# An earlier first projection in the head, and routing that takes the sample tiles first and gathers from the residual stream

## The reference, cut to what matters

```python
mod = jax.nn.silu(cvec) @ p['w_ada'] + p['b_ada']
sh1, sc1, g1, sh2, sc2, g2 = [m[:, None, :] for m in jnp.split(mod, 6, axis=-1)]
h = _rms_norm(x, p['norm1_g']) * (1 + sc1) + sh1
mix, k, v = _mixing(h, p, kv_ctx)
x = x + g1 * mix
h2 = _rms_norm(x, p['norm2_g']) * (1 + sc2) + sh2
x = x + g2 * _expert_choice_ffn(h2, p)

...
logits = (h @ p['w_router']).astype(jnp.float32) + p['b_router'].astype(jnp.float32)
aff = jax.nn.softmax(logits, axis=-1)
gate, idx = lax.top_k(aff.transpose(0, 2, 1), cap)
xs = jax.vmap(lambda hb, ib: hb[ib])(h, idx)
gg = jnp.einsum('becd,edf->becf', xs, p['w_e_gate'])
uu = jnp.einsum('becd,edf->becf', xs, p['w_e_up'])
y = jnp.einsum('becf,efd->becd', jax.nn.silu(gg) * uu, p['w_e_down']) * gate[..., None].astype(h.dtype)
```

## Time and profile before

| | |
|---|---|
| median of three runs | 1210.63 us (1210.62 to 1211.57) |
| profiled execution | 1212.05 us |
| its span | 1209.6 us |
| mean granted TensorE clock | 0.995 |
| PE busy | 1179.1 us, 97% of the span |
| DVE, ACT, POOL busy | 898.7, 613.1, 283.5 us |
| moved by DMA | 303.25 MB, 251 GB/s on average |

### The profile page before, as it was taken

The page is one execution under the profiler, slowest core; times in us unless marked ns, Lnnn a source line. Parts: engine busy times, 40 slices in busy tenths (PEclk is TensorE's granted clock), DMA queues, the critical chain, the costliest instruction groups (busy, mean ns, idle before and its releaser), DMA issues.

```text
span 1209.6 us, 18766 instructions
## 1 busy us (share of the span) xinstructions
PE 1179.1 (97%) x7330; PEld 941.3 (78%) x7330; DVE 898.7 (74%) x1047; ACT 613.1 (51%) x710; POOL 283.5 (23%) x189
## 2 busy tenths in 40 slices
PE   5999999999999999999999999999999999999995
PEld 3788899988899999999995666666666666666663
DVE  2689674558877174237568999999999999999997
ACT  3421332245541351322124777777777777777774
POOL 1131030002201143333126212222222112222213
PEclk9999999999999999999999999999999999999998
DMA  9887726221213123444349999999999999999995
GB/s 339 295 240 234 248 64 157 85 99 35 73 36 105 36 71 100 161 158 153 111 174 369 388 379 378 378 380 381 381 386 389 381 377 378 380 381 380 381 387 202
DMA packets 154762, 303.25 MB, mean 251 GB/s; under 512 B 7363, under 2 KB 55527, under 8 KB 154706
## 3 DMA queue, kind: packets, MB, share of 16 engines
q1 hardware_dynamic: 141942, 271.76, 62.1%
q0 software_dynamic: 3968, 12.64, 4.7%
q10 hardware_dynamic: 8796, 18.05, 4.3%
HBM read 285.25 MB, written 17.18 MB: 250 GB/s over the span
## 4 chain that ended last, share of the span: by engine, by line
PE 90%; DVE 5%; issue 1%; DMA 1%; POOL 1%; ACT 0%; SPq 0%; POOLq 0%; ACTq 0%; DVEq 0%
PE bank L1812 17%; PE bank L1813 17%; PE bank L1814 17%; PE bank L1838 5%; PE bank L1841 5%; PE bank L1843 5%; PE bank L1840 5%; PE bank L1842 5%; PE bank L1839 5%; DVE fa L1236 3%; PE bank L2116 1%; DMA wring<-in_w_ada 1%; DVE fa L1328 1%; PE bank L2099 1%; PE bank L2329 1%
## 5 line engine op out<-in xcount | busy, mean ns | idle before, releaser
L1812 PE MATMUL bank<-h2r_a,xTh 128*80 128x512 f32 x368 | 145.4, 395 | 0.0
L1813 PE MATMUL bank<-l2r_b,xTh 128*80 128x512 f32 x368 | 144.7, 393 | 0.0
L1814 PE MATMUL bank<-h2r_a,xTl 128*80 128x512 f32 x368 | 143.4, 390 | 0.0
L693 POOL TENSOR_TENSOR half<-half 1x1 f32<-1x1 f32 x26 | 60.2, 2316 | 287.6 <-DVE ye L1772 286.6
L1236 DVE SCALAR_TENSOR_TENSOR fa<-fa,cwT 128x655 f32<-128x655 f32 x120 | 111.1, 967 | 0.9
L1058 ACT CAST h2r_a<-w_a 128x2048 fp32r<-128x2048 f32 x46 | 88.1, 1914 | 42.9 <-PE bank L1814 42.9
L589 POOL TENSOR_TENSOR lring<-wring,hring 128x2048 fp32r<-128x2048 f32 x15 | 70.2, 4681 | 162.5 <-ACT hring L752 162.5
L1623 DVE TENSOR_TENSOR l2r_b<-w_a,h2r_a 128x2048 fp32r<-128x2048 f32 x45 | 102.8, 2284 | 5.8 <-ACT h2r_a L1058 5.5
L1838 PE MATMUL bank<-hTh,hring 128*128 128x320 f32 x320 | 104.4, 326 | 1.7 <-DVE hTl L1296 0.8
L1843 PE MATMUL bank<-hTh,lring 128*128 128x320 f32 x320 | 98.8, 309 | 0.0
L1841 PE MATMUL bank<-hTl,hring 128*128 128x320 f32 x320 | 98.8, 309 | 0.0
(11 more groups left out here) (433 smaller groups left out, 3205.4 us busy)
## 6 DMA issues: line engine op xcount, KB each, us to landing
w_b<-in_w_e_down SPq DMA_DIRECT2D x48, 1024.0 KB, 14.8
w_e<-in_w_e_up SPq DMA_DIRECT2D x32, 1024.0 KB, 16.8
w_r<-in_w_e_gate SPq DMA_DIRECT2D x32, 1024.0 KB, 16.9
w_a<-in_w_e_gate SPq DMA_DIRECT2D x32, 1024.0 KB, 14.6
w_a<-in_w_e_up SPq DMA_DIRECT2D x32, 1024.0 KB, 14.3
wring<-in_w_in SPq DMA_DIRECT2D x20, 1024.0 KB, 5.1
w_a<-in_w_e_down SPq DMA_DIRECT2D x16, 1024.0 KB, 14.1
fa<-in_w_ada SPq DMA_DIRECT2D x14, 1024.0 KB, 9.0
```

Source lines behind the costliest of these rows:

```text
L1812: pe.matmul(out, lh, rh, start=start, stop=False)
L1813: pe.matmul(out, lh, rl, start=False, stop=False)
L1814: return pe.matmul(out, ll, rh, start=False, stop=stop)
```

## The change

It has two parts that do not touch each other.

**Head.** The order on PE is written anew: pair turns 0 and 1 come after turn 3, `turn_x(6)` before `ada(4)`, the first chunk before `ada(5)` and the second before `ada(6)`. The low half of the first weights is made in two pieces (`first_lo(rows)` on DVE, a quarter and three quarters), with the first chunk of `hTl` between them, and the first chunk no longer waits for the whole. ACT casts the first chunk of `hTh` before it copies the last two of `xT`.

**Routing.** The last jobs are ordered so that the four sample tiles end before the prompt. Their turns and routes go inside the output jobs (a function called after a given step of `token_major`), ACT takes over the copies of the second halves of the last three tiles, and samples and prompt have a softmax each. The samples are ranked first, from one bank. Expert 0's rows are gathered from `X2` instead of `h2t`, by columns that hold the inverse root in place of ones (`rows_r`, `rows_rp`), and scale and shift are applied while the gathered rows are copied out of PSUM: chunks 0 to 3 on ACT, 4 to 7 on DVE. `xTh` and `xTl` of expert 0 are then made from that copy. POOL scales and shifts tile 4 and the prompt after the samples' softmax, tile 4 first, and ACT stores the prompt's `h2t` after `x_hi_first`.

```diff
-WARM_0, WARM_A, WARM_B = 14, 1, 6
+WARM_A, WARM_B = 3, 3
-OUT_LAST = [(2, 0), (2, 1), (3, 0), (2, 2), (3, 1), (2, 3), (3, 2), (2, 4), (3, 3), (3, 4)]
+OUT_LAST = [(2, 0), (2, 1), (3, 0), (2, 2), (3, 1), (2, 3), (3, 2), (3, 3), (2, 4), (3, 4)]
@@ SP, unit 9 of expert 0 @@
-                        sp.wait_ge(s_gx, 2)
+                        sp.wait_ge(e_xt, 2)
@@ POOL @@
-            for i in range(3):
+            for i in range(4):
                 rstd2(i)
+            gp.wait_ge(s_aff, 1)
             scaled(3)
-            rstd2(3)
+            shifted(3)
             rstd2(4)
             scaled(4)
-            gp.wait_ge(s_aff, 1)
-            for i in (4, 3):
-                shifted(i)
+            shifted(4)
@@ ACT @@
             sum_squares(4)
-            normalise(3)
-            softmax_exp()
-            normalise(4)
+            second_half(4)
             store_x(4)
             e_hi_unit(0, 2)
-            store_h(4)
-            e_hi_unit(0, 3)
-            store_h(3)
+            prompt_exp()
             for hf in range(2):
                 act.wait_ge(s_gx, hf + 1)
                 act.copy(parts[:, 512 * hf:512 * hf + 512], bank[4 + hf][:, :]).then_inc(s_gs, 1)
+            normalise(4)
+            store_h(3)
             def x_raw():
+                act.wait_ge(e_xt, 1)
+                for c in range(4):
+                    for g, cols in ((1, slice(0, CAP_S)), (0, slice(CAP_S, M_E))):
+                        ins = act.activation(x0f[:, c, cols], bank[6][:, c * M_E + cols.start:c * M_E + cols.stop], ACT.Identity,
+                                             bias=col40[:, 16 + 8 * g + c:17 + 8 * g + c], scale=a2c[:, g, c:c + 1])
+                    ins.then_inc(e_xr, 1)
+            def x_hi_first():
+                act.wait_ge(e_xr, 4)
+                act.copy(xTh[:, 0:4, :], x0f[:, 0:4, :]).then_inc(e_xh, 1)
+                act.wait_ge(s_idx, 5)
+                act.copy(xTh[:, 4:8, :], x0f[:, 4:8, :]).then_inc(e_xh, 1)
             x_raw()
+            act.wait_ge(s_hst[0], 16)
+            act.wait_ge(s_hst[1], 16)
+            x_hi_first()
+            store_h(4)
+            e_hi_unit(0, 3)
             e_hi_unit(0, 4)
-            act.wait_ge(s_hst[0], 32)
-            x_hi(0)
@@ DVE, expert 0 @@
+            def x_lo_first():
+                for hf in range(2):
+                    dve.wait_ge(e_xh, hf + 1)
+                    dve.tensor_tensor(xTl[:, 4 * hf:4 * hf + 4, :], x0f[:, 4 * hf:4 * hf + 4, :],
+                                      xTh[:, 4 * hf:4 * hf + 4, :].bitcast(F32), ALU.subtract).then_inc(e_xl, 1)
@@ PE, after the job n = 5 of OUT_LAST @@
+            last_out(6, (3, lambda: route(1, 0)))
+            turn_x2(1, 1)
+            last_out(7, (4, third_tile))
+            last_out(8, (3, fourth_tile))
+            last_out(9, (1, sample_turns))
+            sample_rows(0)
+            turn_x2(1, 4)
+            warm(WARM_A, 1)
+            route(1, 4)
+            sample_rows(1)
```

More of the change, by code:

```diff
@@ new lines, in _ @@
+            dve.tensor_tensor(hot, slot_p.unsqueeze(1).to_broadcast([P, TT - 1, CAP_S]),
+                              rank[:, 1:TT].unsqueeze(2).to_broadcast([P, TT - 1, CAP_S]), ALU.is_equal)
+            dve.wait_ge(s_affp, 2)
+            ranks(0, bank[0][:, 0:P], 0)
+            link(dve.tensor_reduce(rank[:, 0:1], above[:, 0, :], AX, ALU.add))
+            dve.scalar_tensor_tensor(rows_rp, slot_p[:, 0:CAP_P], rank[:, 0:1], stat[:, 10:11].to_broadcast([P, CAP_P]), ALU.is_equal,
+                                     ALU.mult).then_inc(s_idx, 1)
@@ new lines, in _, with x_raw @@
+            dve.tensor_tensor(hot_p, slot_p[:, 0:CAP_P], rank[:, 0:1].to_broadcast([P, CAP_P]), ALU.is_equal).then_inc(s_idx, 1)
+            dve.wait_ge(s_affp, 3)
+            link(dve.tensor_copy(affT, bank[1][0:96, 0:256]))
+            def x_raw():
+                dve.wait_ge(e_xt, 2)
+                for c in range(4):
+                    for g, cols in ((1, slice(0, CAP_S)), (0, slice(CAP_S, M_E))):
+                        ins = dve.tensor_scalar(x0f[:, 4 + c, cols], bank[7][:, c * M_E + cols.start:c * M_E + cols.stop],
+                                                a2c[:, g, 4 + c:5 + c], col40[:, 20 + 8 * g + c:21 + 8 * g + c], ALU.mult, ALU.add)
+                ins.then_inc(s_idx, 1)
@@ L1913, in _ @@
             pe.wait_ge(s_xhat, TT)
-            for dc in range(4):
-                turn_x(dc)
+            turn_x(0)
+            turn_x(1)
             ada(3)
+            turn_x(2)
+            turn_x(3)
             pe.wait_ge(s_cast, 2)
@@ L1934, in _ @@
             chunk()
+            ada(5)
+            chunk()
             ada(6)
-            chunk()
             ada(7)
@@ L2022, in token_major @@
                                dc == DC - 1)
+                    if between is not None and dc == between[0]:
+                        between[1]()
                 last.then_inc(s_job, 1)
@@ L2246, in last_out @@
                     out_unit(3)
-                token_major("out", u, TILE_ORDER[i], out_2 + u - 2)
+                token_major("out", u, TILE_ORDER[i], out_2 + u - 2, between)
             last_out(0)
@@ L2311, in _ @@
                 for c in range(4):
-                    last = pe.matmul(bank[6 + hf][:, c * M_E:c * M_E + CAP_S], parts[:, (4 * hf + c) * P:(4 * hf + c + 1) * P], twice,
+                    pe.matmul(bank[6 + hf][:, c * M_E:c * M_E + CAP_S], parts[:, (4 * hf + c) * P:(4 * hf + c + 1) * P], twice,
                                      start=True, stop=True)
-                last.then_inc(e_xt, 1)
+            warm(WARM_B, 2)
+            pe.wait_ge(s_idx, 3)
+            for c in range(DC):
+                x0 = (c % 4) * M_E + CAP_S
+                last = pe.matmul(bank[6 + c // 4][:, x0:x0 + CAP_P], X2[:, 0, c * P:(c + 1) * P], rows_rp, start=True, stop=True)
+                if c % 4 == 3:
+                    last.then_inc(e_xt, 1)
             def first_lists():
+                pe.wait_ge(s_idx, 4)
                 pe.matmul(bank[3][CAP_S:M_E, 0:2], hot_p, aff[:, 0, 0:2 * E_N:E_N], start=True, stop=True)
```

213 lines of the change are left out of this document (114 added, 99 removed).

## The result

The changed kernel takes 1213.85 us (median of 13 runs, 1212.92 to 1215.97), the kernel before 1210.69 us in the 13 runs beside it. The ratio of the two is 1.0021, with an interval of 1.0014 to 1.0029: about 2.5 us slower (the two medians lie 3.2 us apart; this text goes by the ratios). The span of the profiled execution grew from 1209.6 to 1212.0 us. Forecast were 1212.5 us with a range of 1207.9 to 1217.0, so +1.9 us; the measured difference is larger by 0.6 us by the ratio and by 1.3 us by the medians, and lies at the edge between "within 0.2%" and "slower".

The account below looks back on a forecast made before the run. PE was taken to bound the kernel (90% of the chain), with the weight stream also full. Head -1.1 us and store +3.0 us, using up the routing's 1.95, gave +1.9: 1212.5 us, range 1207.9 to 1217.0.

Parts of the forecast that it names:

- Head: PE's idle stretches of 0.77 and 0.35 us in the head go: 1.1 us gained, between 0 and 1.16.
- Up to unit 0: Routing: last output job ends at 631.0 us, expert 0's unit 0 starts at 644.0 in place of 645.95, 1.95 us earlier.
- The low end of 642.75 us: Earliest start named for expert 0's unit 0, if all the work moved ahead is gained.
- The store: Prompt's store, issued at 646.0 us, lands at 653.1 and gates POOL's low halves; unit 4 starts at 662.4, 3.0 us later.
- The reading of the earlier trace: POOL's unit 3 low half waited for a store landing at 648.3 us; the named ACT cast was unit 4's.
- about 2.6 us lower: The sum if the store took the 3.4 us estimated from the skill's page and landed at 649.4 us.
- DVE behind POOL: First rival: store lands before 652.4 us, `xTl` is caught behind POOL at expert 0; 1213 to 1217 us; chance 0.22.
- The sum: Head's -1.1 us plus the store's +3.0 us: +1.9 us, 1212.5 us on the median.
- The gate is not the store: Faster rival: the store does not hold POOL, routing keeps 0.7 to 1.95 us; 1208.8 to 1207.6 us; chance 0.23.
- No head gain: Rival: first chunks only move the wait, or unit 4's stall is 1 us; parts cancel, 1210 to 1211.5 us; chance 0.10.
- the first part of the prediction: PE bounds the kernel; the weight stream is full too, so a large gain would run into it, a loss not.
- PE's idle time should cost no clock: In the routing, 628 to 646 us, PE idles 1.38 us at granted clock 1.00, so no clock loss was expected.

Follow-up runs that it names:

- the two runs that moved its start: Changed kernel with the prompt's store behind a wait for unit 3's cast: 1.0039; or issued ahead of ACT's scalings, `xTl` and unit 7 also earlier: 0.9988.
- the head's run: The kernel before with only the change's hunks on the head: ratio 0.9990 to before (0.9981 to 0.9999).
- the two runs that differ in unit 7 alone: Changed kernel, POOL's wait for the prompt's store moved behind unit 4's low half, `xTl` behind the second search: 1.0015; with unit 7 fetched one output job earlier: 0.9975.
- POOL's wait moved: Changed kernel with POOL's wait for the prompt's store moved from ahead of unit 3's low half to behind unit 4's: ratio 1.0039 to before.
- the store behind the cast's end: Changed kernel with the prompt's store behind unit 3's cast on ACT and a wait for that cast's end: ratio 1.0039 to before.
- `xTl` earlier alone: Changed kernel with only DVE's two `xTl` subtractions moved from behind the fifth search to behind the second: ratio 1.0016 to before.
- unit 7 early alone: Changed kernel with only unit 7 of expert 0's weights fetched one output job earlier: ratio 1.0018 to before.
- the fastest kernel: Changed kernel with POOL's wait moved, `xTl` behind the second search and unit 7 fetched one output job earlier: 1209.04 us, ratio 0.9975 to before.

## Why the prediction was right

**Head.** Predicted 1.1 us: 0.92 at the row of chunks, 1.2 on the whole with an interval of 0.1 to 2.3. The first chunk came 2.0 us earlier, where 1.5 to 2 was named, and the runs without the routing or without the head show the gain carried to unit 4. A wait of 0.58 us ahead of a later turn is new, behind ACT's copy, which the sum had not seen.

**Up to unit 0.** Predicted 1.95 us earlier on the clock of before; 2.72 less the head's 0.92 is 1.80. The last job ends at 630.4 us (the end of PE's work ahead of its wait for the first ranks), 3.6 us later on that clock, where the sum had 3.2. The low end of 642.75 us that was named for unit 0 does not follow from the terms, which give 631.0 + 12.4 = 643.4 with no wait at all; on that clock unit 0 came at 644.15, and the 644.0 held.

**The store.** On the clock of before it was to be issued at 646.0, to land after 7.1, and to let unit 4 start at 662.4. It was issued at 645.34 + 0.92 = 646.3, landed after 6.9, and unit 4 started at 661.58 + 0.92 = 662.5. That the start fits so well is in part luck, since two errors in it cancel: the eight scalings on DVE took 1.91 us where the sum had 1.4, and the store did not wait for the 0.38 us of the cast, with which it started. Behind the longer scalings `xTl` ended at 653.17 on that clock, where 652.6 was named, and PE had a first wait of 1.16 us at unit 2 that the sum did not have; unit 4, which POOL sets, did not move by it. The reading of the earlier trace rows, that the row's named cast was not the releaser, held. The rule of the Trainium skill, "DMA: Bandwidth & Descriptors", section "Anatomy of one DMA — SWDGE (gpsimd) path", would have given some 3.4 us, an estimate from its fixed part and the bytes; but that section is about transfers that GpSimd starts, and this store is started by ACT. The prompt's store took 6.9 us in the change, and 7.5 and 7.1 in the two runs that moved its start, so the measurement decides. Nor would a sum "about 2.6 us lower" follow from a landing at 649.4 us: by the prediction's own first rival, that landing starts POOL ahead of `xTl`, and DVE is caught.

**The sum.** -1.1 + 3.0 was +1.9; the rows say -0.92 + 3.3 = +2.4, and the time +2.5 by the ratio. The two terms were mis-sized by 0.2 and 0.3 us, both to the same side.

**The rivals.** *DVE behind POOL* was right as a mechanism and missed its condition by 0.14 us in the change, and by 0.07 us with the routing alone (`xTl` ended at 653.16 us, POOL started at 653.23). That the forecast held and not this rival is therefore in part luck too. Where POOL was freed the rival struck at once, and cost 6.3 us of waiting and a stretch at half clock. *The gate is not the store* is out by the two runs that moved the store. *No head gain* is out by the head's run, if narrowly, and by unit 4 in the run without the head's part. What the first part of the prediction said in passing, that a large gain would run into the weight stream while a loss would not, is shown by the two runs that differ in unit 7 alone, 1.0015 and 0.9975; the sentence was right, but I had not priced that the change itself starts the stream 2.5 us later.

**Where the wording was too wide.** "PE's idle time should cost no clock" held for the change (4.45 us in three waits, granted clock 1.00), and not for five other kernels here, in which one wait was between 2.24 and 6.33 us. The idle time that it was read from, 1.38 us in 628 to 646 us of the kernel before, was three short waits of 0.35, 0.68 and 0.35 us.

## What to carry to other kernels

When a tile is produced earlier but its store is written later in an engine's program, look for whoever counts that store: here a buffer's wait counted all stores where it needed those of two tiles. A gain on the busiest engine has to be followed to the end of the run: the transfers that start behind the same job have moved too, and only when both were freed did the change show. Before moving a DVE operation's input from PSUM to SBUF, look at what POOL runs at that time, and place the operation where POOL is idle rather than trust to a margin of 0.14 us.

## What was unexpected

A transfer written behind a cast in ACT's program was started at 645.18 us, 0.36 us before that cast began; with a wait for the semaphore that the cast sets at its end, it started at 647.43.

PE ran at the lower of its two clock levels (granted 0.50) behind single waits of 6.33 us (658 to 664 us, with POOL's wait moved), 4.10 us (659 to 665 us, the store behind the cast's end), 3.49 us (1191.0 to 1197.5 us, ahead of the last unit) and 3.04 us (657 to 660 us, `xTl` earlier alone), and with unit 7 early alone behind a wait of 2.24 us that followed one of 1.16 us (658 to 661 us). Behind the change's waits of 1.16, 1.75 and 1.55 us the granted clock stayed at 1.00. The unit 3 of the kernel with unit 7 early, and its window:

```profile
656.94 0.46 PE L1883 MATMUL bank<-h2r_a,xTh 128*80 128x512 f32 x1 [2.24 <-POOL l2r_b L684]
```

```profile
646.00:663.00 17.00, 13.60 (x49) 6.75 (x48) 15.86 (x38) 6.28 (x6) 9.08 (x2) 0.90 1.03 375
```

The twelve matmuls of the unit behind the wait of 4.10 us took 5.20 us (659.22 to 664.42) against 3.22 in the fastest kernel (652.68 to 655.90, a wait of 0.3 us included). What that costs depends on who waits: there unit 4 started 0.75 us behind POOL's low half, while with unit 7 early, where unit 3 took 4.52 us, it started within 0.05 us of the low half (661.46 us against 661.41), and nothing was lost by it.
